# Shared expert at step 3, from two fixed loads in pieces 18 and 19 of the ring, and the second half of the output projection loaded ahead of the shift rows

## The reference

```python
def _moe(h, w_router, router_bias, w_expert_gate_up, w_expert_down, w_shared_gate_up, w_shared_down):
    scores = jax.nn.sigmoid((t @ w_router).astype(jnp.float32))
    ...                                   # group-limited choice of 8 of 64 experts per token
    gu = jnp.einsum('td,edf->etf', t, w_expert_gate_up)      # 64 experts, 1024 -> 2 x 256
    g, u = jnp.split(gu, 2, axis=-1)
    act = jax.nn.silu(g) * u * combine.T[:, :, None]
    routed = jnp.einsum('etf,efd->td', act, w_expert_down)   # 64 experts, 256 -> 1024
    sg, su = jnp.split(t @ w_shared_gate_up, 2, axis=-1)     # the shared expert: all tokens
    shared = (jax.nn.silu(sg) * su) @ w_shared_down
    return routed + shared
out = (g_a * y_a + g_b * y_b) @ w_out                        # the output projection, before the MoE
xf = x + gate1 * out ;  h = _rmsnorm(xf, norm2_g) * (1.0 + scale2) + shift2
```

## Time and profile before

| | us |
|---|---|
| median of 3 runs (lowest, highest) | 825.35 (824.7, 827.12) |
| the profiled execution | 827.55 |
| its span | 825.6 |
| TensorE busy | 783.9 (95% of the span) |
| VectorE busy, ScalarE busy | 380.0, 236.0 |
| loaded and stored | 284.74 MB, mean 345 GB/s |

### The profile page before, as it was taken

The page is one execution under the profiler, slowest core; times in us unless marked ns, Lnnn a source line. Parts: engine busy times, 40 slices in busy tenths (PEclk is TensorE's granted clock), DMA queues, the critical chain, the costliest instruction groups (busy, mean ns, idle before and its releaser), DMA issues.

```text
span 825.6 us, 13387 instructions
## 1 busy us (share of the span) xinstructions
PE 783.9 (95%) x5490; PEld 531.8 (64%) x5490; DVE 380.0 (46%) x773; ACT 236.0 (29%) x400; POOL 21.9 (3%) x22
## 2 busy tenths in 40 slices
PE   4999999999999999999999999899999999999974
PEld 1779897999999999956356355354554845455222
DVE  1176999889998654673323322121221112122114
ACT  2173747444354453231111111021111101011001
POOL 1000010100100100200000000000000000000000
PEclk9999999999999999999999999899999999999997
DMA  8998898633634299869999999999999999999994
GB/s 331 408 372 321 293 396 317 198 109 104 199 109 168 92 331 379 331 272 426 387 426 428 425 427 427 426 427 427 426 426 422 427 425 426 427 425 426 429 417 165
DMA packets 73159, 284.74 MB, mean 345 GB/s; under 512 B 5256, under 2 KB 12040, under 8 KB 48392
## 3 DMA queue, kind: packets, MB, share of 16 engines
q1 hardware_dynamic: 72600, 282.55, 85.5%
q10 hardware_dynamic: 496, 1.30, 0.4%
HBM read 280.67 MB, written 3.16 MB: 344 GB/s over the span
## 4 chain that ended last, share of the span: by engine, by line
PE 65%; SPq 15%; DMA 10%; DVE 5%; issue 2%; ACT 2%; POOL 0%; DVEq 0%; POOLq 0%; ACTq 0%
PE bank L2120 15%; SPq L630 11%; PE bank L2176 8%; DMA chunk<-in_w_expert_down 6%; PE bank L1731 5%; PE bank L1733 5%; PE bank L1736 5%; PE bank L2027 4%; PE bank L2004 4%; PE bank L1717 3%; PE bank L1775 3%; PE bank L1678 2%; DMA ring<-in_w_out 2%; PE bank L1996 2%; DMA ring<-in_w_ada 2%
## 5 line engine op out<-in xcount | busy, mean ns | idle before, releaser
L2120 PE MATMUL bank<-chunk,xg 128*64 128x512 f32 (+2 forms) x1024 | 196.9, 602 | 8.2 <-DMA chunk<-in_w_expert_gate_up 8.0
L2120 PEld LDWEIGHTS bank<-chunk,xg 128*64 128x64 f32 (+2 forms) x1024 | 62.2, 127 | 136.5 <-issue 120.7
L2176 PE MATMUL bank<-chunk,act_t 128*64 128x512 f32 (+2 forms) x480 | 97.4, 613 | 1.8 <-DMA chunk<-in_w_expert_down 1.8
L1529 DVE SCALAR_TENSOR_TENSOR act_r<-bank,w_slot,sil 128x256 f32<-128x256 f32 x26 | 12.6, 484 | 165.4 <-ACT sil L997 165.4
L1542 DVE TENSOR_TENSOR y_lo<-bank,y_hi 128x512 fp32r<-128x512 f32 x52 | 35.9, 692 | 77.1 <-ACT y_hi L1010 77.1
L997 ACT ACTIVATE sil<-bank 128x256 f32<-128x256 f32 x26 | 10.0, 385 | 194.0 <-PE bank L2120 194.0
L1092 DVE TENSOR_TENSOR ring_lo<-ring,ring_hi 128x1024 fp32r<-128x1024 f32 x44 | 52.9, 1221 | 22.0 <-ACT ring_hi L779 21.9
L2176 PEld LDWEIGHTS bank<-chunk,act_t 128*64 128x64 f32 (+2 forms) x480 | 30.0, 129 | 48.4 <-issue 47.6
L1010 ACT ACTIVATE y_hi<-bank 128x512 fp32r<-128x512 f32 x52 | 30.9, 597 | 105.4 <-PE bank L2176 97.6
L1152 DVE SCALAR_TENSOR_TENSOR conv<-upad,dw,conv 128x256 f32<-128x256 f32 x120 | 52.8, 514 | 0.0
L779 ACT ACTIVATE ring_hi<-ring 128x1024 fp32r<-128x1024 f32 x44 | 44.4, 1052 | 27.1 <-PE bank L1757 12.6
(11 more groups left out here) (316 smaller groups left out, 1178.0 us busy)
## 6 DMA issues: line engine op xcount, KB each, us to landing
chunk<-in_w_expert_gate_up SPq DMA_DIRECT2D x128, 1024.0 KB, 24.8
chunk<-in_w_expert_down SPq DMA_DIRECT2D x63, 1024.0 KB, 25.7
ring<-in_w_in SPq DMA_DIRECT2D x16, 2048.0 KB, 10.1
ring<-in_w_ada SPq DMA_DIRECT2D x12, 2048.0 KB, 9.6
ring<-in_w_proj_hgrn SPq DMA_DIRECT2D x2, 2048.0 KB, 7.8
ring<-in_w_out SPq DMA_DIRECT2D x2, 2048.0 KB, 13.8
ring<-in_w_proj_conv SPq DMA_DIRECT2D x1, 2048.0 KB, 8.9
chunk<-in_w_shared_gate_up SPq DMA_DIRECT2D x2, 1024.0 KB, 27.1
```

The lines of the kernel that those rows point to most:

```text
L2120: ins = mm(bank[2 + b][row:row + width, :], xg[:, k, c:c + width], w[:, k % 4, :], start=(k == 0), stop=(k == KD - 1))
L2176: ins = mm(out[row:row + width, :], act_t[:, c, row:row + width], w[:, c, h * 512:(h + 1) * 512], start=(c == 0), stop=(c == 1))
```

## The change

There are two parts.

1. `SHARED_STEP, SHARED_DOWN` go from 18, 20 to 3, 4. The shared expert's gate and up become pieces 18 and 19, its down projection piece 32, and the ranked experts' pieces begin with number 20. Pieces 18 and 19 need no routing, so SP issues them ahead of its wait for `order_done`. VectorE makes the shared expert's input in steps 1 and 2, two parts in each. The wait of the gather for `act_s_done` is put where the odd step needs it.
2. `load_block("wo1")` goes from ahead of fixed piece 8 to ahead of the shift rows and fixed piece 5.

```diff
--- before.py
+++ after.py
@@ -63,7 +63,7 @@
 
 NCHUNK = 20
 EARLY_CHUNKS = 2
-SHARED_STEP, SHARED_DOWN = 18, 20
+SHARED_STEP, SHARED_DOWN = 3, 4
 CHUNK_NO = {}
 for n_step, n_items in enumerate(ITEMS_OF):
     if n_step == SHARED_STEP:
@@ -590,6 +590,7 @@
 
             for number in range(EARLY_CHUNKS, 3 * FIXED):
                 if number == 5:
+                    load_block("wo1")
                     sp.wait_ge(o_ready, 4)
                     sp.wait_ge(s_g2_kept, 16)
                     for s in range(NS):
@@ -597,7 +598,6 @@
                 if number == 7:
                     sp.wait_ge(ob_used, 4)
                 if number == 8:
-                    load_block("wo1")
                     released(sp, "ph1")
                 if number == 12:
                     released(sp, "wo0")
@@ -629,17 +629,21 @@
                     src, dst = gu_src[bass.ds(e, 1)][:, :, 4 * part:4 * part + 4, :].rearrange("a p k f -> (a p) k f"), gu_tile(place)
                 sp.dma_start(dst, src).then_inc(s_chunk[place], 16)
 
-            sp.wait_ge(order_done, 1)
             for step in range(FIXED_STEPS, NSTEPS):
                 if step == SHARED_STEP:
                     for half in range(2):
                         number = CHUNK_NO["shared gate and up", half]
-                        freed(number - NCHUNK)
+                        if number == NCHUNK - 1:
+                            sp.wait_ge(s_x1_kept, 16)
+                            sp.wait_ge(x1_sq, 5)
+                            sp.wait_ge(g_done, 5)
                         sp.dma_start(gu_tile(place_of(number)), cols(A["w_shared_gate_up"][0], 0)[:, 4 * half:4 * half + 4, :]).then_inc(s_chunk[place_of(number)], 16)
                 if step == SHARED_DOWN:
                     number = CHUNK_NO["shared down"]
                     freed(number - NCHUNK)
                     sp.dma_start(dn_tile(place_of(number)), A["w_shared_down"][0].rearrange("(c p) d -> p c d", p=P)).then_inc(s_chunk[place_of(number)], 16)
+                if step == FIXED_STEPS:
+                    sp.wait_ge(order_done, 1)
                 experts = []
                 for part in range(3):
                     for item in range(ITEMS_OF[step]):
@@ -647,13 +651,7 @@
                             j = FIRST_ITEM[step] + item
                             experts.append(sp.value_load(e_row[0:1, j:j + 1], min_val=0, max_val=NE - 1))
                         number = CHUNK_NO[step, part, item]
-                        if number < NCHUNK:
-                            if number == NCHUNK - 1:
-                                sp.wait_ge(s_x1_kept, 16)
-                                sp.wait_ge(x1_sq, 5)
-                                sp.wait_ge(g_done, 5)
-                        else:
-                            freed(number - NCHUNK)
+                        freed(number - NCHUNK)
                         if number < len(CHUNK_NO) - 1:
                             load_ranked(place_of(number), part, experts[item])
                             continue
@@ -1579,8 +1577,9 @@
                     n_extra = dve.value_load(nwork, min_val=0, max_val=NX)
                 if n:
                     result_lo(b, n)
-                if 2 <= n < 6:
-                    shared_input(n - 2)
+                if 1 <= n < 3:
+                    shared_input(2 * n - 2)
+                    shared_input(2 * n - 1)
 
             def extra_pair(b, i, more):
                 gate(b, i * 2 + b)
@@ -2102,6 +2101,7 @@
                 pe.wait_ge(pt_evac, i * 2 + 2)
                 if isinstance(i, int) and i == SHARED_STEP // 2:
                     pe.wait_ge(sg_done, 1)
+                    pe.wait_ge(act_s_done, 1)
                 gather(0)
                 pe.wait_ge(gbk_evac, i * 2 + 2)
                 gather(1)
@@ -2157,8 +2157,6 @@
 
             def second_turn(i, weights):
                 pe.wait_ge(pt_evac, i * 2 + 1)
-                if isinstance(i, int) and i == SHARED_STEP // 2:
-                    pe.wait_ge(act_s_done, 1)
                 turn(1, weights)
 
             def act_to_channels(b, p):
```

## The result

| | before | changed |
|---|---|---|
| median, us (lowest, highest) | 825.77 (824.7, 827.12) | 838.34 (837.74, 838.57) |
| ratio to before, 95% interval | | 1.0152 [1.0133, 1.0171] |
| the profiled execution, us | 827.55 | 838.57 |
| span, us | 825.6 | 836.6 |

The changed kernel is 12.6 us slower by the medians (1.5%); the prediction was 837.8 us, with a range of 830.5 to 840.4. It was worked out from 825.35, the median of three executions of the kernel before; with a fourth that median is 825.77. First two rows of the page of the changed kernel: the same work (TensorE is busy 3 us more; the megabytes are the same 284.74), but slice 21 of the GB/s row, 418 to 439 us, has fallen to 179.

What follows compares the result with a forecast made beforehand. Transfers bound the kernel, TensorE nearly balanced. Terms -4.96, +1.0 (later stream start), +2.65 and +13.9 sum to 12.6; followed by piece, 12.4 later, 840 profiled, 837.8 us as median; range 830.5 to 840.4.

Steps and rivals of the forecast that it cites:

- What bounds the kernel: From about 420 us to the end: transfers never pause and set the end, nearly balanced with TensorE, which waits for them.
- wo1, 1.20 us: Ahead of step 0: wo1 issued at 304.0 instead of 311.48 removes TensorE's 1.20 us wait, so step 0 begins at 360.94.
- Two pieces early, -4.96, and the longer first pause, +2.65: Pieces 18 and 19 loaded ahead take 4.96 us off the stream; its pause near 391 to 395 grows from 1.75 to 4.4.
- The second pause, 13.9 us: Step 3: piece 38 needs the place shared_up holds, so the stream stops from 415.0 to 428.9.
- the wait on the input: Ahead of shared_up in step 3: TensorE stands 4.5 us until VectorE's last shared_input calls end at 411.4.
- The clock, 1.7 us: In shared_up, behind the wait on the input: a lower clock costs 1.7 us, bounds 0 and 3.4.
- 157 pieces at 2.481 us: From 428.9 us to the end: pieces 38 to 194 take 2.481 us each, ending at 818.4.
- The tail, "the same": Behind the last piece, at the end of the kernel: the tail is the same as in the kernel before.
- Its own range, 835.5 to 839.7: Whole kernel: the forecast, chance 0.70, with the clock at 0 or 3.4 instead of 1.7 and 0 to 1.2 for wo1.
- The first rival: Whole stream, ledger of bytes alone: two megabytes leave the saturated stream, nothing pauses; -4.0 us, 821.4 us, chance 0.04.
- the pause at 395: Kernel before: the stream pauses 1.75 us, read by a rule on repeated gaps as a want of places in the ring.
- the third: Step 3: the ring starves without a 4.5 us input wait or slow clock; second pause 7.7 us, 831.6 us, chance 0.12.

Runs made afterwards that it cites:

- The doubled work: The 64 matmuls of the shared gate and up done twice: at step 3 in the changed kernel, 853.55 us; at step 18 in the kernel before, 829.86 us.
- the pieces not early: The changed kernel, but SP waits for the order of the experts ahead of pieces 18 and 19, so both load after the routing; 838.16 us.
- the shared expert alone: The changed kernel with wo1 loaded where it was before, the shared expert still at steps 3 and 4; 839.97 us.
- the input in time: The changed kernel, but VectorE makes three parts of the shared expert's input ending step 1, the fourth in step 2 ahead of the transposed copy; 830.85 us.
- changed, shared_up twice at 3: The changed kernel with the 64 matmuls of the shared gate and up done twice in step 3; 853.55 us.
- wo1 alone: The kernel before with only wo1 loaded ahead of the shift rows, the shared expert staying at steps 18 and 20; 824.21 us.
- wo1, shared expert at 4 and 5: The kernel before with wo1 early, the shared expert at steps 4 and 5, no early pieces, its input made in time in steps 1 and 2; 827.76 us.
- wo1, shared expert at 8 and 10: The kernel before with wo1 early and the shared expert at steps 8 and 10 instead of 18 and 20, nothing loaded early; 823.77 us.

## Why the prediction was right, step by step

- **What bounds the kernel: shown.** The doubled work shows it from both sides. The transfers set the end, and in the kernel before TensorE has only some 9 us of slack behind step 18. As the prediction had it, the waits for loads at 523 and 533 vanish; in the changed kernel TensorE waits for no load from 428 us until this one:

```profile
679.62 5.34 PE L2174 MATMUL bank<-chunk,act_t 128*32 128x512 f32 x32 [2.85 <-DMA chunk<-in_w_expert_down]
```

- **wo1, 1.20 us: right.** The wait went; step 0 began 1.38 us earlier in the traces (360.76 for 362.14), the time moved by 1.2 alone and 1.6 with the other part. The shift rows, behind it in the queue, took 8.18 us to issue instead of 4.91 and landed in 13.0 and 15.5 us, by about 322; TensorE reads them only from 348.3 on.
- **Two pieces early, -4.96, and the longer first pause, +2.65: right in sum, rough in form.** The 4.4 us that I put at 391 to 395 came as 3.0 us of pause (215 and 382 of 427 GB/s in the two windows from 390 to 400) and 1.2 us of thinner stream (374 GB/s over 370 to 380, where the kernel before has 425). That both together are worth nothing is shown by the kernel that loads them late and takes the same time.
- **The second pause, 13.9 us: right.** Measured 14.5 us. Its parts: the wait on the input 4.5 (4.48), `shared_up` 14.1 (14.08 without the wait ahead of it).
- **The clock, 1.7 us: too small.** 16.85 - 14.08 = 2.8 us in this trace, inside the bounds of 0 and 3.4. The window 410 to 415 has a granted clock of 0.51, about the 1.2 GHz level, 415 to 420 one of 0.81, a mean of the two levels. Other traces with the same wait have 1.7 us (15.74, the pieces not early) and 2.4 (16.48, the shared expert alone). That the sum came within 0.6 us of the median is in part luck: this term was 1.1 us short, and the tail, below, 1.7 us too long.
- **157 pieces at 2.481 us: right.** The last piece was used at 818.65, predicted 818.4. From 429.7 on that is (818.65 - 429.7) / 157 = 2.477.
- **The tail, "the same": off by 1.7 us in the profiled pair.** Before, the last down projection was a slow group, 5.34 us; after, it was not:

```profile
809.98 5.04 PE L2120 MATMUL bank<-chunk,xg 128*32 128x512 f32 x32 [3.02 <-DMA chunk<-in_w_expert_gate_up]
818.65 3.67 PE L2188 MATMUL bank<-chunk,act_t 128*32 128x512 f32 x32 [1.37 <-DMA chunk<-in_w_expert_down]
```

That is why the spans differ by 11.0 us and the last pieces by 12.7. The trace with the pieces not early has it the other way round, as the kernel before does:

```profile
807.65 3.64 PE L2119 MATMUL bank<-chunk,xg 128*32 128x512 f32 x32 [2.57 <-DMA chunk<-in_w_expert_gate_up]
...
816.36 5.34 PE L2187 MATMUL bank<-chunk,act_t 128*32 128x512 f32 x32 [2.80 <-DMA chunk<-in_w_expert_down]
```

What the two groups have to do with each other is told in the last section.

Three places of the prediction do not hold in themselves, though the forecast did not hang on them. Its own range, 835.5 to 839.7, does not follow from the terms it names: the clock at 0 gives 836.1, and the clock at 3.4 with nothing from wo1 gives 840.7. The first rival was said to gain something with a second pause of under about 8 us; by the prediction's own terms (-4.96 + 1.0 + 2.65) the limit is 1.3 us, and the kernel with the input in time, whose pause is 7.3 us, is 5.4 us slower than the kernel before. And the pause at 395 in the kernel before stands alone, it is not a gap that repeats; that it is a want of places rests on SP's order, in which piece 30 waits for the place of piece 10.

Of the rivals, the third (no late input) named its time, 831.6, and the kernel with the input in time measured 830.85. That TensorE is the bound is refuted as the cause here. It is near all the same: the 14 us added at step 18 used up its 9 us of slack.

Not settled: why the stream delivered 374 GB/s instead of 425 while its DMA share stood at 1.00 (370 to 380). In all four kernels that load pieces 18 and 19 early it was 365 to 374, in the six that load them behind the routing 424 to 428. The changed kernel and the one with the pieces not early issue the next pieces at nearly the same times (364.61, 365.78, 368.89, 370.00, 374.54 and 363.74, 364.90, 368.02, 369.11, 373.67), but in the second two more pieces stand in the queue ahead of them. That points to the short queue; how it thins the stream no run shows. Nor did any run vary the queue's depth alone: that depth makes the place of the shared expert matter is argued from steps 3, 4 and 8, where other work changes with it.

## What to carry to other kernels

With a ring of buffers a load is early only if there is a place for it. Follow the ring piece by piece: which matmuls free the place that the next load needs, and is there other work put in front of them? Work that frees nothing belongs where many issued loads are queued: 14 us of it were no dearer at step 8 than at step 18. Where few are queued it stops the stream for what the queue does not cover (7.3 of 14.08 us at step 3), and whatever comes on top counts in full (13.75 us for 14.08 when it was doubled); the stream, saturated from there to the end, did not give it back. Look also at how near the next limit is: the same 14 us added at step 18 did not stop the stream and still cost 4.95 us, since TensorE had only 9 us of slack. And moving the consumer of a value forward moves the due time of its producer: here two calls of `shared_input`, 3.1 us of VectorE, cost 7.3 us, 4.5 of wait and 2.8 of lower clock behind it.

## What the runs showed of the hardware that was not expected

**The same wait, two clocks.** The first gather of the routing stage stands behind the same wait of 0.99 to 1.00 us in every trace. It ran at full clock in four of them. In five the granted clock over 356 to 358 us had a mean of 0.50 to 0.53, and in the kernel before with the doubled work it was slow too (its matmuls took 3.23 and 2.54 us, where the fast ones took 2.17 and 1.12 + 1.22). Step 0 of the changed kernel then began at 360.76, and with the pieces not early, at full clock, at 359.89.

**A slow group that costs nothing, and the fast one that does.** The last gate and up and the last down projection that TensorE waits for are groups of 32 matmuls, each 3.6 us at full clock. In nine of the ten traces it waits ahead of both (us):

| kernel | wait, last gate and up | its matmuls | wait, last down | its matmuls |
|---|---|---|---|---|
| changed, shared_up twice at 3 | 2.41 | 3.64 | 4.05 | 5.14 |
| changed, 18 and 19 not early | 2.57 | 3.64 | 2.80 | 5.34 |
| before | 2.67 | 3.64 | 2.81 | 5.34 |
| wo1 alone | 2.69 | 5.34 | 1.09 | 3.66 |
| wo1, shared expert at 4 and 5 | 2.91 | 5.07 | 1.33 | 3.67 |
| changed | 3.02 | 5.04 | 1.37 | 3.67 |
| changed, input in time | 3.26 | 5.06 | 1.39 | 3.67 |
| shared expert alone | 3.71 | 6.47 | 0.56 | 3.66 |
| wo1, shared expert at 8 and 10 | 3.97 | 5.34 | 1.10 | 3.66 |

Either the gate and up is slow and the down projection fast, or the other way round, in all nine. The last piece comes when the stream brings it. A slow gate and up mostly fills time in which TensorE would wait for it, and the last group then follows a short wait at full clock (with the shared expert alone the slow group was so long that the 0.56 us are a wait for ScalarE). A fast one leaves a wait of 2.8 us or more, and behind it the last group is slow, 1.5 to 1.7 us that nothing hides. So two kernels whose last pieces come at the same time can differ by 1.7 us. That the wait's length decides is argued from these rows; it was not varied by itself, and elsewhere in the kernel before two groups were slow behind waits of only 2.22 and 1.76 us.

The executions of the kernel before spread from 823.8 to 828.9 us. So a time from one profile is good to a few us only, and the medians decide below that.
